# Modulation of a two-stage network on one core: the shift of layer 0 by matmuls, the rest by multiply-and-sum chunks on VectorE; layer norms at full width

## The reference

```python
for l in range(DEPTH):                       # DEPTH = 2
    mod = c @ w_ada[l] + b_ada[l]            # c: (1, 1024), w_ada[l]: (1024, 3072)
    shift, scale, gate = jnp.split(mod, 3, axis=-1)
    h = _layer_norm(x, LN_EPS) * (1.0 + scale[:, None, :]) + shift[:, None, :]
    proj = h @ w_in[l]                       # then attention, short convolution, Fourier mixing -> y
    y = jnp.concatenate([y_attn, y_conv, y_four], axis=-1) @ w_out[l]
    x = _layer_norm(DEEPNORM_ALPHA * x + (1.0 + gate[:, None, :]) * y, LN_EPS) * ln_g[l] + ln_b[l]
# second block, each layer: feed-forward, mixer, feed-forward, each on an rms norm of x and with one behind it
hh = _rmsnorm(x, norm_w[i, 0])
x = x + FFN_RES * _rmsnorm(_swiglu(hh, w_gate, w_up, w_down), norm_w[i, 1])
```

## Time and profile before

| | |
|---|---|
| median of 3 runs | 3008.81 us (3007.4 to 3012.82) |
| the profiled execution | 3008.55 us, of which the span of the trace is 3006.8 us |
| TensorE busy | 2838.2 us, 94% of the span |
| VectorE busy | 1456.4 us, 48% |
| ScalarE busy | 1023.1 us, 34% |
| granted TensorE clock, mean | 0.96 |
| loaded and stored | 245.02 MB |

### The profile page before, as it was taken

The page is one execution under the profiler, slowest core; times in us unless marked ns, Lnnn a source line. Parts: engine busy times, 40 slices in busy tenths (PEclk is TensorE's granted clock), DMA queues, the critical chain, the costliest instruction groups (busy, mean ns, idle before and its releaser), DMA issues.

```text
span 3006.8 us, 38616 instructions
## 1 busy us (share of the span) xinstructions
PE 2838.2 (94%) x16220; PEld 2225.1 (74%) x16220; DVE 1456.4 (48%) x2103; ACT 1023.1 (34%) x1526; POOL 1.4 (0%) x6
## 2 busy tenths in 40 slices
PE   5999999998999999979999999999999879899998
PEld 1476577657888877768788887888877568688886
DVE  1148444754533456454454345533455676454344
ACT  0035434543322335412432223322234432332222
POOL 0000000000000000000000000000000000000000
PEclk9999989997999999899899999999999899899998
DMA  9221112111323222100122323223232100122322
GB/s 387 85 70 64 49 56 77 64 49 50 108 85 110 79 85 96 41 32 29 64 92 88 109 80 96 98 83 110 78 95 77 57 22 4 57 91 84 109 81 70
DMA packets 65116, 245.02 MB, mean 81 GB/s; under 512 B 7216, under 2 KB 7344, under 8 KB 63536
## 3 DMA queue, kind: packets, MB, share of 16 engines
q1 hardware_dynamic: 64656, 238.36, 23.5%
q0 software_dynamic: 288, 4.19, 0.4%
HBM read 240.43 MB, written 2.10 MB: 81 GB/s over the span
## 4 chain that ended last, share of the span: by engine, by line
PE 91%; DVE 4%; ACT 3%; issue 1%; DMA 1%; SPq 0%; ACTq 0%; DVEq 0%
PE bank L367 89%; ACT work L1392 1%; DVE work L1961 1%; PE bank L550 1%; DMA work<-w_ada 1%; ACT weights_high L1426 1%; DVE residual L1961 1%; DVE weights_low L1975 0%; ACT normed L1392 0%; ACT silu_gate L1392 0%; ACT L1392 0%; PE bank L1150 0%; DVE work L2348 0%; DVE work L2650 0%; DVE silu_gate L2664 0%
## 5 line engine op out<-in xcount | busy, mean ns | idle before, releaser
L367 PE MATMUL bank<-normed,weights_high 128*128 128x512 f32 x4848 | 1544.1, 400 | 25.6 <-ACT normed L1392 22.0
L367 PEld LDWEIGHTS bank<-normed,weights_high 128*128 128x128 f32 x4848 | 914.8, 191 | 252.3 <-issue 62.3
L367 PE MATMUL bank<-normed,weights_low 128*128 128x512 f32 x2424 | 957.4, 395 | 0.0
L1975 DVE TENSOR_TENSOR weights_low<-ring,weights_high 128x1024 fp32r<-128x1024 f32 (+2 forms) x431 | 483.9, 1126 | 526.1 <-ACT weights_high L1426 522.8
L1426 ACT ACTIVATE weights_high<-ring 128x1024 fp32r<-128x1024 f32 (+2 forms) x431 | 420.7, 979 | 931.4 <-PE bank L367 931.3
L367 PEld LDWEIGHTS bank<-normed,weights_low 128*128 128x128 f32 x2424 | 463.4, 191 | 98.8
L367 PE MATMUL bank<-hidden,weights_high 128*128 128x512 f32 x1408 | 433.4, 389 | 0.0
L367 PEld LDWEIGHTS bank<-hidden,weights_high 128*128 128x128 f32 x1408 | 264.3, 188 | 54.8
L2190 DVE TENSOR_TENSOR silu_gate<-bank,rstd 128x512 f32<-128x512 f32 x176 | 120.9, 691 | 340.8 <-PE bank L367 336.0
L367 PE MATMUL bank<-hidden,weights_low 128*128 128x512 f32 x704 | 273.9, 389 | 0.0
L367 PE MATMUL bank<-work 64*64 64x64 f32 (+7 forms) x1632 | 161.2, 320 | 4.2 <-DVE work L2650 3.2
(11 more groups left out here) (222 smaller groups left out, 1897.7 us busy)
## 6 DMA issues: line engine op xcount, KB each, us to landing
ring<-w_k SPq DMA_DIRECT2D x303, 512.0 KB, 3.2
work<-w_ada SPq DMA_DIRECT2D x6, 4096.0 KB, 20.9
ring<-w_d SPq DMA_DIRECT2D x64, 384.0 KB, 3.0
ring<-w_d SPq DMA_DIRECT2D x64, 320.0 KB, 2.9
work<-dft_in POOLq DMA_DIRECT2D x2, 2048.0 KB, 8.1
constants<-cst_in SPq DMA_DIRECT2D x1, 2304.0 KB, 8.0
residual<-x_in SPq DMA_DIRECT2D x1, 2048.0 KB, 13.3
out_dram<-residual SPq DMA_DIRECT2D x8, 256.0 KB, 2.0
```

The costliest lines, as they stand in the source:

```text
L367: return pe.matmul(o, lhsT, rhs, start=start, stop=stop, skip_group_check=True)
L1975: ve.tensor_tensor(WL[:, u % SPLIT, 0:w], RING[:, u % SLOTS, 0:w], WH[:, u % SPLIT, 0:w].bitcast(F32), ALU.subtract).then_inc(unit_split, 1)
```

## The change

- SyncE's order becomes: vectors, the first 256 columns of the constants (identity and the matrix of 1/1024, moved to the front), the residual, four quarters of layer 0's shift piece, units 0 and 1, a copy of c on all partitions (512 KB), eight chunks of 512 KB of layer 0's scale piece, units 2 and 3, the rest of the constants, the small weights.
- TensorE makes the mean of the first layer norm first, then half of the shift row, the sum of squares, the other half of the row, and its columns.
- The other five pieces are stored transposed, with an output feature per partition. A chunk holds 128 output features: 128x1024 weights. VectorE multiplies it by the copy of c and sums along the row in one instruction (`ada`), into one column of `MOD`. Layer 0's scale (8 chunks) is made between the first norm's reciprocal and its first scaled tile; the 32 chunks of the other four pieces in the slots of the first projection of layer 0: three each in slots 0 to 8 and 14, two in slot 15.
- GpSimd loads these 32 chunks into four buffers, each when the chunk that held its buffer is consumed.
- The low halves of units 0 to 2 are made between the first norm's steps, that of unit 3 after it; ScalarE makes the high halves after the norm's root.
- Layer norms and feed-forward norms are taken at full width: the sum of squares is a matmul of the constant matrix into a whole bank (8 for a layer norm, 1 for a feed-forward norm), root and reciprocal are of 128x512, and there is no spread and no copy of it. The norms behind feed-forwards and mixers and ahead of mixers stay as they are (`compact`).

```diff
+        def compact(norm):
+            return norm[0] == "post" or norm[0] == "pre" and norm[1].startswith("mix")
...
+        def scale_chunk(u):
+            return GATE[:, 0:2, :] if u == 7 else BIG[:, (24, 26, 28, 30, 16, 18, 20)[u]:(26, 28, 30, 32, 18, 20, 22)[u], :]
+        def ada_chunk(m):
+            return BIG[:, 24 + 2 * (m % 4):26 + 2 * (m % 4), :]
...
+            early = 2 * P
+            sp.dma_start(VEC[:], vec_in).then_inc(vectors_in, 16)
+            sp.dma_start(CST[:, 0:early], cst_in[:, 0:early]).then_inc(start_in, 16)
+            sp.dma_start(X[:], x_in).then_inc(start_in, 16)
+            for i in range(4):
+                sp.dma_start(BIG[:, 32 + 4 * i:36 + 4 * i, :], w_shift[:, 4 * i:4 * i + 4, :]).then_inc(shift_in[i], 16)
...
+            for u in range(2):
...
+            sp.dma_start(BIG[:, 22:24, :], c_in).then_inc(c_copies_in, 16)
+            for u in range(KT):
+                sp.dma_start(scale_chunk(u), w_ada[0][:, 2 * u:2 * u + 2, :]).then_inc(scale_in[u], 16)
+            for u in range(2, SLOTS):
+                load(u, "k", u)
+            sp.dma_start(CST[:, early:NC], cst_in[:, early:NC]).then_inc(consts_in, 16)
+            sp.dma_start(SMALL[:], small_in).then_inc(consts_in, 16)
...
+            pool.wait_ge(w_loaded[SLOTS - 1], 16)
+            for m in range(4 * KT):
+                pool.wait_ge(*dve_done("ada", 1 + (m - 4) // KT, (m - 4) % KT) if m >= 4 else dve_done("ada", 0, m))
+                pool.dma_start(ada_chunk(m), w_ada[1 + m // KT][:, 2 * (m % KT):2 * (m % KT) + 2, :]).then_inc(ada_in[m % 4], 16)
...
+            def shift_rows(i):
+                pe.wait_ge(shift_in[i], 16)
+                for k in (2 * i, 2 * i + 1):
+                    for side in range(2):
+                        ins = mm(PS[side][0:1, :], v("c", k), tile(32 + 2 * k + side), start=(k == 0), stop=(k == KT - 1))
+                if i == 3:
+                    step(ins, "modrow")
+            def shift_columns():
+                pe.wait_ge(*dve_done("modrow"))
+                for u in range(KT):
+                    ins = mm(PS[1][:, u:u + 1], GATE[0:1, 2 + u // 4, col(u % 4)], v("one")[0:1])
+                step(ins, "mod")
...
                 mean_over_features(norm, "mean", lambda k: X[:, k, :], PS[6], after)
-                rms_of(norm, *[(tile(k), act_done("sq", norm, k)) for k in range(KT)])
-                spread(norm)
+                if norm == ("ln", 0):
+                    for i in range(2):
+                        shift_rows(i)
+                mean_over_features(norm, "ms", lambda k: tile(k), PS[7], lambda k: act_done("sq", norm, k))
...
+                if l == 0:
+                    pe.wait_ge(consts_in, 32)
...
-                                     lambda x: H[:, KT + x, :], 0, KT, KT, ("pre", f) if q == 0 and j == LEAD + 1 else None)
+                                     lambda x: H[:, KT + x, :], 0, KT, KT)
                         if q == 0 and j == LEAD:
-                            rms_of(("pre", f), (tile(0), dve_done("sum", f)))
+                            pe.wait_ge(*dve_done("sum", f))
+                            step(mm(PS[7][:], cst("onesD"), tile(0)), "ms", ("pre", f))
...
+            pe.wait_ge(vectors_in, 16)
             for l in range(DEPTH):
-                layer_norm(("ln", l), lambda k: dve_done("x", "first", l - 1, k) if l else (consts_in, 64))
+                layer_norm(("ln", l), lambda k: dve_done("x", "first", l - 1, k) if l else (start_in, 32))
+                if l == 0:
+                    for i in range(2, 4):
+                        shift_rows(i)
+                    shift_columns()
...
-                a(RSTD[:, 0, 0:4], PS[7][:, 0:4], ACT.Sqrt, "sd", norm,
+                w = TT if compact(norm) else T
+                a(RSTD[:, 0, 0:w], PS[7][:, 0:w], ACT.Sqrt, "sd", norm,
                   bias=v("eps5" if norm[0] in ("ln", "pln") else "eps6"), chain=False)
...
                         root(("pre", f))
-                        kept_rstd(("pre", f))
...
+            act.wait_ge(vectors_in, 16)
             lru_lambda()
             for l in range(DEPTH):
                 squares(("ln", l))
+                if l == 0:
+                    for u in range(SPLIT):
+                        high(u)
...
-                d(ve.reciprocal(RSTD[:, 0, 4:8], RSTD[:, 0, 0:4]), "rstd", norm, chain=False)
+                if compact(norm):
+                    d(ve.reciprocal(RSTD[:, 0, 4:8], RSTD[:, 0, 0:4]), "rstd", norm, chain=False)
+                else:
+                    d(ve.reciprocal(RSTD[:, 1, :], RSTD[:, 0, :]))
...
+                if norm == ("ln", 0):
+                    shift_row()
+                    low(0)
                 reciprocal_std(norm)
-                dve.wait_ge(*pe_done("spread", norm))
+                if norm == ("ln", 0):
+                    shift()
+                    low(1)
+                    dve.wait_ge(c_copies_in, 16)
+                    for u in range(KT):
+                        ada(1, u)
+                    low(2)
                 for k in range(KT + 1):
                     if k < KT and first:
-                        d(stt(tile(8 + k), tile(8 + k), MOD[:, l, 8 + k:9 + k], PS[7][:], ALU.mult, ALU.mult),
+                        d(stt(tile(8 + k), tile(8 + k), MOD[:, l, 8 + k:9 + k], RSTD[:, 1, :], ALU.mult, ALU.mult),
...
-                dve.wait_ge(*act_done("rstd", ("pre", name)))
+                if compact(("pre", name)):
+                    dve.wait_ge(*act_done("rstd", ("pre", name)))
...
+            def ada(q, u):
+                l, part = divmod(q, 3)
+                dve.wait_ge(*((ada_in[((q - 2) * KT + u) % 4], 16 * (((q - 2) * KT + u) // 4 + 1)) if q > 1 else (scale_in[u], 16)))
+                w = scale_chunk(u) if q == 1 else ada_chunk((q - 2) * KT + u)
+                d(ve.scalar_tensor_tensor(out=w, in0=w, scalar=v("one"), in1=BIG[:, 22:24, :], op0=ALU.mult, op1=ALU.mult,
+                                          accum_out=MOD[:, l, 8 * part + u:8 * part + u + 1]), "ada", q - 1, u,
+                  chain=(u == KT - 1))
+                if u == KT - 1:
+                    m = MOD[:, l, 8 * part:8 * part + 8]
+                    d(stt(m, m, 1.0 if part else 0.0, VEC[:, VCOL["bada"] + 8 * q:VCOL["bada"] + 8 * q + 8], ALU.add, ALU.add),
+                      chain=(q == 1))
+            def shift_row():
+                dve.wait_ge(*pe_done("modrow"))
+                for side in range(2):
+                    d(ve.tensor_copy(GATE[0:1, 2 + side, :], PS[side][0:1, :]), *(("modrow",) if side else ()), chain=False)
+            def shift():
+                dve.wait_ge(*pe_done("mod"))
+                d(ve.tensor_tensor(MOD[:, 0, 0:8], PS[1][:, 0:8], VEC[:, VCOL["bada"]:VCOL["bada"] + 8], ALU.add), "shift0",
+                  chain=False)
             def first_block(l):
@@ -2085,6 +2135,11 @@
...
+                    if l == 0:
+                        if j == K0 + 1:
+                            dve.wait_ge(consts_in, 32)
+                        for m in range(3 * j, 3 * j + 3) if j < 9 else range(27, 30) if j == 14 else range(30, 32) if j == 15 else ():
+                            ada(2 + m // KT, m % KT)
...
+    w_shift = a["w_ada"][0, :, 0:D].reshape(KT, P, 2, T).transpose(1, 0, 2, 3).reshape(P, 16, T)
+    w_ada = np.stack([a["w_ada"][l, :, q * D:q * D + D].T.reshape(KT, P, 2, T).transpose(1, 0, 2, 3).reshape(P, 16, T)
+                      for l in range(DEPTH) for q in range(3) if l or q])
+    c_in = np.broadcast_to(a["c"].reshape(1, 2, T), (P, 2, T))
```

73 lines of the change are left out of this document (14 added, 59 removed).

## The result

The changed kernel takes **2909.94 us** (median of 4 runs, 2909.67 to 2911.08) against 3009.66 for the kernel before (4 runs, 3007.4 to 3012.82); the ratio is 0.9669, 95% interval [0.9654, 0.9683]. The profiled execution took 2909.84, its span is 2907.9, mean granted clock 0.968. 2907 in 2897 to 2929 was forecast.

A forecast was written before the change was run, and what follows sets the result against it. TensorE was taken as the bound, idle at the start until modulation weights land. Sum: 3008.6 - 97.0 (start) + 0.6 (cold start) + 8.0 (slots) - 10.1 (layer norms) - 3.0 (feed-forward norms) = 2907.1, so 2907 us, range 2897 to 2929.

The forecast's parts named there:

- Forecast 60.7: Kernel start: the first projection would begin at 60.7 us instead of 157.7, a gain of 97.0 us.
- +0.6 for the cold start: First projection: TensorE, idle from 43 to 60 us, starts at half pace for some 5 us, against about 4 before.
- (b): Rival, chunks: the summing instruction runs at half rate, 2.4 us a chunk, giving 2951 us; chance 0.07.
- (c): Rival, norms: the full-width sums run at half clock, giving 2927 us; chance 0.08.
- (d): Rival, start: queued loads share the engines rather than run in order; start 10 us later, 2917 us; chance 0.05.
- +8.0 forecast: First projection's slots: VectorE, with chunks added, falls behind and TensorE waits, costing 8.0 us; +5 to +6 with chunks of 1.20.
- the buffers don't limit up to 5.0: Slots: four buffers suffice while a chunk's buffer comes round in about 5 us; 4.4 to 5.3 estimated.
- Rival (a): Slots: chunks come late because a buffer takes T us round; for T = 8, +18 us, 2925; chance 0.12.
- 7T - 29: VectorE's lateness at attention in us if a buffer takes T us round, for T above 6.
- the 15 at which the prediction was to be called wrong: Attention entry: the prediction counts as wrong if VectorE enters attention more than 15 us late.
- -10.1 forecast: Three later layer norms at full width: 11.0 us each to the first scaled tile, gaining 3.0, 2.2 and 4.9 us.
- -3.0 forecast: Four feed-forward norms: two full-width records (0.87 us) replace eight one-column records and eight of the spread, 0.75 us each.

The follow-up runs named there:

- kernel without slot chunks: Changed kernel without the 32 chunks in the first projection's slots and their loads; the gate of layer 0 and layer 1's pieces set to one: 2898.21 us, ratio 0.9640.
- the run with the constants ahead: Changed kernel with the 2176 KB load of the other constants moved back ahead of the residual in SP's queue: 2920.35 us, ratio 0.9703.
- kernel without loads: Changed kernel with the 32 slot chunks' work on VectorE but not their loads, each summing what lies in its buffer: 2905.07 us, ratio 0.9657.
- compact form: Also "compact norms": changed kernel with all layer norms but the first, and the norms ahead of the FFN, in their former form: 2926.47 us, ratio 0.9722.
- scale chunks first: Changed kernel with VectorE's eight scale chunks put ahead of the first norm's reciprocal and the row copies: 2898.71 us, ratio 0.9628.

## Why the prediction was right

**Start.** Forecast 60.7 for the projection's first record, measured 60.85. The residual lands at 10.2 rather than 9.7, the mean takes 9.9 rather than 9.3, the three blocks of records 7.0 to 7.1 rather than 6.9 (row copies 41.17 against 39.7); on the other side the chunk is 1.205, the lower bound, not 1.30, and the bias additions are shorter. Errors of +1.5 and -1.3 cancel, so 60.85 was partly luck. The +0.6 for the cold start had the wrong sign in this execution: from the projection's first record to slot 0 it took 19.06 us against 19.44 before. In the kernel without slot chunks, which has the same start, it took 20.6.

**Rivals (b), (c), (d).** The summing instruction takes 1282 ns for 1024 columns, in step with 751 for 512 without a sum: so (b), half the rate, is out. The rule of the Trainium skill ("Vector Engine (DVE) Microarchitecture Reference", Points that are easy to get wrong), that two SBUF sources wider than bf16 halve it, doesn't agree with this row, and the row decides. (c) is out by the windows at 1.00, (d) by the run with the constants ahead.

**Slots.** Here a term was mis-sized: +8.0 forecast, 14.0 measured up to the largest score, 14.8 up to the second norm. The part for VectorE's work was right: for chunks of 1.20 the forecast had +5 to +6, and the chunk of 1.205 costs 6.4 by the kernel without loads. What failed is the step "the buffers don't limit up to 5.0", with a round trip of 4.4 to 5.3 us. It was worked out from one load of 2048 KB, and it counts the landing alone. The landing took 5.3 to 7.4 us at the start of the slots, and the round of a buffer also holds the chunk itself (1.2) and its issue (0.4): 6.95 us for the first. The loads cost 7.6 us, where nothing was put down for them. Rival (a), which prices this mechanism, was what happened in part. Its formula, 7T - 29, gives 14.4 us of lateness at attention for the 6.2 of the first nine loads and 12.3 for 5.9, the median of all 27; VectorE's largest score was 14.0 late. That it comes so near is partly luck, as T has to be read as the landing: with the whole round of 6.95 it gives 19.7. I gave it 0.12 and priced it at T = 8 alone; with T at 6.2 it adds (14.4 - 0.8 - 8.0 =) 5.6, and the sum would have been near 2913. Of the signs set down, waits of VectorE for loads in slots 0 to 7 did show, and its lateness at attention stayed 1 us below the 15 at which the prediction was to be called wrong. TensorE's waits for the heads came to 7.2 us for the 4.4 forecast, that for the first probabilities to 3.35.

**Layer norms.** -10.1 forecast; 2.7, 1.9 and 4.65 measured from sum of squares to first tile, 9.2 in all, where the forecast had 3.0, 2.2 and 4.9. The three parts of the new form (7.13, 0.69, 3.35) were right to 0.25.

**Feed-forward norms.** -3.0 forecast. Undone, they give about 1.3, 2.4, 0.5 and 1.1, sum 5.3. In the trace with the compact form the two groups take 0.95 and 1.05 against one of 1.02, 1.0 each, so 4 of the 5.3 are explained; I did not settle the rest. The forecast of 0.75 took the price of the eight records from the earlier trace rows with their overlap at both ends.

**What made the sum come out.** Against the profiled execution the start brought 0.9 more than forecast (97.3 for 96.4), the slots lost 6.8 more, the norms brought 1.0 less and the rest of the kernel 4.3 more: 2.6 together, where 2909.84 is 2.7 above 2907.1. In that rest lie the two mixers, which the change doesn't touch: between equal landmarks of the two traces they are 4.1 longer and 3.9 shorter. So the total was nearer than its terms, and that was luck: 6.8 us of loss missing in the slots and 1.0 too much gain in the norms stood against 5.2 of gain missing at the start and in the rest of the kernel. Of the 4.3 in the rest 2.3 are the feed-forward norms; about 2 were not traced.

## What to carry to other kernels

Work that an idle engine takes over has to be placed by the slack of its whole stretch: 32 chunks of 1.2 us cost 14.0 us with their loads as first placed, and nothing when they had more buffers, seven of them went into an idle gap and one instead of eight lay in the stretch from slot 8 to attention. A buffer ring is to be sized by its whole round (the work on the buffer, the issue and the landing in traffic), not by the landing of one load: here four buffers lost 7.6 us, six 1.3 and twelve none. And an engine's queue should be read for what waits in it for others: the reciprocal and the chunks in another order were worth 13.4 us at the start, with not one instruction less.

## What was not expected of the hardware

The accumulator's write-out on VectorE is a record of 82 ns (mean of 39) that overlaps the next instruction: chunks of 1.28 us follow one another at 1.205 us with it in between. On ScalarE it took 0.19.

Unchanged code takes several us more or less by the granted clock. Between the same two small reciprocals a stretch of the first mixer took 163.9 us in the kernel before, 169.2 in the changed one and (169.1 to 169.3) in nine of the experiments, 163.8 with the scale chunks first, 166.7 with compact norms. The whole stretch in the kernel before, the changed kernel and the one with the scale chunks first:

```profile
1261.41:1425.34 163.93, 146.90 (x1643) 123.11 (x1644) 75.60 (x113) 43.91 (x76) 0.00 (x0) 0.94 0.10 33
```
```profile
1167.44:1336.62 169.18, 152.20 (x1643) 126.85 (x1644) 75.57 (x113) 43.90 (x76) 0.00 (x0) 0.91 0.10 32
```
```profile
1157.15:1320.94 163.79, 146.88 (x1643) 123.17 (x1644) 75.62 (x113) 43.90 (x76) 0.00 (x0) 0.94 0.10 33
```

The records are the same in number, and length times granted clock is 154.0 us in the last two and 154.1 in the first. The second mixer ran between 349.4 and 353.5 us. What ahead of it decides this I did not find: no experiment varied it alone. My estimate from these stretches (5.4 and 4.1 us between the extremes) is that a sum of terms can't promise more than some 4 us for this kernel.
